# HGRN layer: one tile of i's projection moved into each of the first seven state tiles

## What is computed

```
def hgrn2_mixer(h, w_in, lb, onorm_g, w_out):       # H = 8 heads of 128, chunks C = 64
    q, fl, i, g = split(h @ w_in, 4)
    q = silu(q); f = lb + (1 - lb) * sigmoid(fl); k = 1 - f; logf = log(f)
    b = cumsum(logf, within a chunk)
    q_dec, k_inv, k_state = q * exp(b), k * exp(-b), k * exp(b_last - b)
    A = causal(q_dec @ k_inv.T)                      # scores, 64 x 64 in a chunk
    o_intra = A @ i                                  # products from the scores
    U = k_state.T @ i                                # state products
    S_next = exp(b_last) * S + U                     # state updates, chunk after chunk
    o = o_intra + q_dec @ S                          # products with the states
    o = o * rsqrt(mean(o * o) + eps) * onorm_g       # over the 128 values of a head
    return (o * silu(g)) @ w_out
```

## Time and profile before

| | us |
|---|---|
| median of three runs | 3572.93 (3567.02 to 3577.70) |
| the profiled execution | 3579.63 |
| its span, first to last instruction | 3577.8 |
| PE busy | 3427.7 (96%) |
| DVE busy | 1945.3 (54%) |
| ACT busy | 1275.9 (36%) |

### The profile page before, as it was taken

How to read it: one execution, slowest core, us unless ns; L and a number is a source line. 1 busy time by engine, 2 the same in 40 slices (tenths; PEclk the granted TensorE clock), 3 DMA queues, 4 the chain that set the end, 5 groups by cost and what they waited for, 6 DMA issues and landing times.

```text
span 3577.8 us, 54525 instructions
## 1 busy us (share of the span) xinstructions
PE 3427.7 (96%) x22697; PEld 2834.6 (79%) x22697; DVE 1945.3 (54%) x2638; ACT 1275.9 (36%) x1638; POOL 13.9 (0%) x20
## 2 busy tenths in 40 slices
PE   9999999999999999899999999999899887999998
PEld 7778888887788878677887788887887885888887
DVE  4566636436574654575344665344676666755434
ACT  3474424334443332353222443223532113633223
POOL 0000000000000000000000000000000000000000
PEclk9999999999899999999999999999999999999999
DMA  4102222221122222112222222222234001123222
GB/s 158 59 1 94 96 101 96 94 94 48 55 99 94 94 94 97 59 59 94 95 94 94 94 71 94 94 96 92 94 106 142 16 5 45 54 83 104 96 94 71
DMA packets 50429, 297.06 MB, mean 83 GB/s; under 512 B 6847, under 2 KB 7871, under 8 KB 17348
## 3 DMA queue, kind: packets, MB, share of 16 engines
q1 hardware_dynamic: 39376, 269.92, 22.1%
q10 hardware_dynamic: 10868, 24.41, 1.9%
HBM read 283.99 MB, written 10.33 MB: 82 GB/s over the span
## 4 chain that ended last, share of the span: by engine, by line
PE 85%; DVE 9%; ACT 4%; issue 2%; ACTq 0%; DMA 0%; DVEq 0%
PE PS L353 13%; PE PS L355 13%; PE PS L354 13%; PE PS L478 7%; PE PS L480 7%; PE PS L479 7%; PE PS L2153 2%; PE PS L2154 2%; PE PS L2155 2%; PE PS L2678 1%; PE PS L2681 1%; PE PS L2671 1%; PE PS L3170 1%; PE PS L3171 1%; PE PS L3172 1%
## 5 line engine op out<-in xcount | busy, mean ns | idle before, releaser
L172 DVE TENSOR_TENSOR WL<-W,WH 128x2048 fp32r<-128x2048 f32 x249 | 570.6, 2292 | 681.2 <-ACT WH L162 675.6
L162 ACT ACTIVATE WH<-W 128x2048 fp32r<-128x2048 f32 x249 | 476.3, 1913 | 1058.5 <-PE PS L480 553.8
L353 PE MATMUL PS<-XH,WH 128*128 128x512 f32 x2080 | 812.8, 391 | 4.2 <-issue 4.2
L355 PE MATMUL PS<-XH,WL 128*128 128x512 f32 x2080 | 810.2, 389 | 0.0
L354 PE MATMUL PS<-XL,WH 128*128 128x512 f32 x2080 | 810.1, 389 | 0.0
L353 PEld LDWEIGHTS PS<-XH,WH 128*128 128x128 f32 x2080 | 390.9, 188 | 91.1 <-issue 10.6
L354 PEld LDWEIGHTS PS<-XL,WH 128*128 128x128 f32 x2080 | 390.9, 188 | 81.8 <-issue 1.0
L355 PEld LDWEIGHTS PS<-XH,WL 128*128 128x128 f32 x2080 | 390.8, 188 | 81.2
L752 DVE TENSOR_TENSOR PS<-PS,R 128x512 f32<-128x512 f32 x248 | 171.0, 696 | 432.4 <-PE PS L355 422.7
L478 PE MATMUL PS<-HH,WH 128*128 128x512 f32 (+1 forms) x960 | 374.8, 390 | 1.2
L480 PE MATMUL PS<-HH,WL 128*128 128x512 f32 (+1 forms) x960 | 373.8, 389 | 0.0
(11 more groups left out here) (509 smaller groups left out, 4761.7 us busy)
## 6 DMA issues: line engine op xcount, KB each, us to landing
W<-in_weights SPq DMA_DIRECT2D x254, 1024.0 KB, 4.9
gate_spill<-slots ACTq DMA_DIRECT2D x16, 256.0 KB, 2.0
gates<-gate_spill ACTq DMA_DIRECT2D x2, 2048.0 KB
x_spill<-X ACTq DMA_DIRECT2D x1, 2048.0 KB, 7.8
X<-x_spill ACTq DMA_DIRECT2D x1, 2048.0 KB
out<-X ACTq DMA_DIRECT2D x8, 256.0 KB, 2.1
W<-in_weights SPq DMA_DIRECT2D x2, 512.0 KB, 5.3
X<-in_x ACTq DMA_DIRECT2D x4, 256.0 KB, 7.7
```

What stands on the lines that cost most here:

```text
L162: P.e.activation(K.WH[:, s, :], K.W[:, s, :], ACT.Copy).then_inc(P.sem("hi_ready"), P.adds("hi_ready"))
L172: P.e.tensor_tensor(K.WL[:, s, :], K.W[:, s, :], K.WH[:, s, :].bitcast(F32), ALU.subtract).then_inc(P.sem("weights_split"), P.adds("weight ...
L353: P.e.matmul(out, wh[:, k, c], xh[:, k, r], start=(k == 0), stop=False)
L355: last = P.e.matmul(out, wl[:, k, c], xh[:, k, r], start=False, stop=(k == KT - 1))
```

## The change

The stages `Store` for i and `Hgrn` become one stage, `HgrnHalf`. Its PE program begins with one tile of i's projection (`AHEAD = 8` steps of three matmuls). Then come the eight state tiles. The table `FILL` says for each state tile how many steps stand at five places in it; for the first seven tiles it is eight steps at the third place, between the state products and the products from the scores. For this the rest is put in another order:

- i's projection has two banks of its own (1 and 4), each used again for every second tile; `scaled` on DVE takes the finished tile and only then makes the next tile's keys.
- PE turns over the keys first, then multiplies the scores, then takes the mean, and only then turns over i, in the bank in which the scores stood, so behind their mask. The keys and the mean share bank 2.
- ACT takes the output of a tile at the start of the next one, squares first, then copies; it copies the keys before i.
- Norm, high and low part of the output come one tile behind instead of two.
- The weight panels are split at the end of every second state tile (`panel_end`). The first tile's scan, exponentials and keys are no longer made ahead of the stage.
- The logs have one row instead of eight, and the output's high and low part lie in other memory (`o_hi`, `o_lo`), since XH and XL are still read.

The core of the diff:

```
-class Hgrn(Stage):
-    tiles_given = 8
+class HgrnHalf(Wide):
+    between_panels = True
+    tiles_given = 8
+    DENSE, MEANS = (1, 4), 2
+    FILL = ((0, 0, 8, 0, 0),) * 7 + ((0, 0, 0, 0, 0),)
+    AHEAD = 8
...
     def dve(self, K, P):
+        def scaled(j):
+            P.e.wait_ge(P.sem("tile_done"), P.due("tile_done"))
+            P.e.tensor_tensor(K.i1[:, j, :], K.PS[:, self.DENSE[j % 2], 0:S], K.RB[:, :], ALU.mult).then_inc(P.sem(f"tile_evacuated{j % 2}"), 1)
...
+        decays(0)
+        keys(0)
+        scaled(0)
         for t in range(8):
-            if t >= 2:
-                normed(t - 2)
+            masked(t)
             if t < 7:
                 decays(t + 1)
-            masked(t)
-            if t >= 2:
-                low_part(t - 2)
+            if t:
+                normed(t - 1)
             states(t)
             if t < 7:
+                scaled(t + 1)
                 keys(t + 1)
+            if t:
+                low_part(t - 1)
+            if t % 2 == 0:
+                panel_end()
...
     def act(self, K, P):
+        logs(0)
+        exps(0)
         logs(1)
         for t in range(8):
+            if t:
+                taken(t - 1)
             turned(t)
-            if t >= 2:
-                high_part(t - 2)
-            if t >= 1:
+            if t:
                 root(t - 1)
             if t < 7:
                 exps(t + 1)
             if t < 6:
                 logs(t + 2)
-            taken(t)
+            if t:
+                high_part(t - 1)
+            if t % 2 == 0:
+                panel_end()
...
     def pe(self, K, P):
+        def fill(steps):
+            for _ in range(steps):
...
+                if k == 0:
+                    if t == 0:
+                        P.e.wait_ge(P.sem("weights_split"), P.due("weights_split"))
+                    P.e.wait_ge(P.sem(f"tile_evacuated{t}"), P.due(f"tile_evacuated{t}", less=-1 if p else 0))
...
+                P.e.matmul(out, wh[:, k, c], K.XH[:, k, 0:S], start=(k == 0), stop=False)
+                P.e.matmul(out, wh[:, k, c], K.XL[:, k, 0:S], start=False, stop=False)
+                last = P.e.matmul(out, wl[:, k, c], K.XH[:, k, 0:S], start=False, stop=(k == KT - 1))
...
+        fill(self.AHEAD)
         for t in range(8):
...
-            for c in tiles:
-                last = P.e.transpose(K.PS[:, 0, c], K.i1[:, t, c], K.ident[:, :])
-            last.then_inc(P.sem("iT_done"), P.adds("iT_done"))
             P.e.wait_ge(P.sem("keys_ready"), P.due("keys_ready"))
+            if t >= 2:
+                P.e.wait_ge(P.sem("o_root"), P.due("o_root"))
...
             last.then_inc(P.sem("A_done"), P.adds("A_done"))
-            P.e.wait_ge(P.sem("iT_ready"), P.due("iT_ready"))
+            fill(fills[0])
             P.e.wait_ge(P.sem("ksT_ready"), P.due("ksT_ready"))
+            if t:
+                means(t - 1)
+            P.e.wait_ge(P.sem("A_ready"), P.due("A_ready"))
+            input_there(t)
+            for c in tiles:
+                last = P.e.transpose(K.PS[:, 0, c], K.i1[:, t, c], K.ident[:, :])
+            last.then_inc(P.sem("iT_done"), P.adds("iT_done"))
+            fill(fills[1])
+            P.e.wait_ge(P.sem("iT_ready"), P.due("iT_ready"))
...
             last.then_inc(P.sem("U_done"), P.adds("U_done"))
+            fill(fills[2])
             if t:
-                means(t - 1)
-            P.e.wait_ge(P.sem("A_ready"), P.due("A_ready"))
+                P.e.wait_ge(P.sem("o_taken"), P.due("o_taken"))
...
+            fill(fills[3])
             P.e.wait_ge(P.sem("states_ready"), P.due("states_ready"))
...
             last.then_inc(P.sem("o_done"), P.adds("o_done"))
+            fill(fills[4])
```

More of the change, by code:

```diff
@@ L1348, in decays @@
         P.e.wait_ge(P.sem("logf_ready"), P.due("logf_ready"))
-        P.e.tensor_tensor_scan(K.h_b[:, :], K.reset64[:, :], self.log_row(K, t), 0.0, ALU.mult, ALU.add).then_inc(P.sem("b_ready"), P.adds("b_ready"))
+        P.e.tensor_tensor_scan(K.h_b[:, :], K.reset64[:, :], K.lf[:, :], 0.0, ALU.mult, ALU.add).then_inc(P.sem("b_ready"), P.adds("b_ready"))
     def keys(self, K, P, t):
@@ L1360, in keys, with panel_end @@
         P.e.tensor_tensor(ks, ki, ends, ALU.mult).then_inc(P.sem("keys_ready"), P.adds("keys_ready"))
[L1362 to L1384, removed]
     def dve(self, K, P):
         decays, keys = lambda t: self.decays(K, P, t), lambda t: self.keys(K, P, t)
+        def scaled(j):
+            P.e.wait_ge(P.sem("tile_done"), P.due("tile_done"))
+            P.e.tensor_tensor(K.i1[:, j, :], K.PS[:, self.DENSE[j % 2], 0:S], K.RB[:, :], ALU.mult).then_inc(P.sem(f"tile_evacuated{j % 2}"), 1)
+        def panel_end():
+            split_dve(K, P)
+            P.split_left -= 1
+            P.count("tile_evacuated0", 1)
+            P.count("tile_evacuated1", 1)
+            P.parity ^= 1
         def masked(t):
             P.e.wait_ge(P.sem("A_done"), P.due("A_done"))
-            P.e.tensor_tensor(K.aT[:, :], K.PS[:, 4, 0:256], K.causal64[:, 0:256], ALU.mult).then_inc(P.sem("A_ready"), P.adds("A_ready"))
+            P.e.tensor_tensor(K.aT[:, :], K.PS[:, 0, 0:256], K.causal64[:, 0:256], ALU.mult).then_inc(P.sem("A_ready"), P.adds("A_ready"))
         def states(t):
@@ L1445, in root @@
             P.e.wait_ge(P.sem("o_mean"), P.due("o_mean"))
-            P.e.activation(r, K.PS[:, 1, :], ACT.Ln, bias=K.eps_col[:, 0:1]).then_inc(P.sem("act_order"), P.adds("act_order"))
+            P.e.activation(r, K.PS[:, self.MEANS, :], ACT.Ln, bias=K.eps_col[:, 0:1]).then_inc(P.sem("act_order"), P.adds("act_order"))
             P.e.wait_ge(P.sem("act_order"), P.due("act_order", 0))
@@ L1452, in taken, with panel_end @@
             for u in range(2):
-                P.e.activation(K.halves(K.o_sq[:, t % 2, :], u), K.halves_ps(u), ACT.Square)
+                last = P.e.activation(K.halves(K.o_sq[:, t % 2, :], u), K.halves_ps(u), ACT.Square)
+            last.then_inc(P.sem("squares_ready"), P.adds("squares_ready"))
+            for u in range(2):
                 last = P.e.activation(K.halves(K.f1[:, t, :], u), K.halves_ps(u), ACT.Copy)
-            last.then_inc(P.sem("squares_ready"), P.adds("squares_ready"))
+            last.then_inc(P.sem("o_taken"), P.adds("o_taken"))
         def high_part(t):
             P.e.wait_ge(P.sem("o_gated"), P.due("o_gated"))
-            P.e.activation(K.XH[:, t, 0:S], K.f1[:, t, :], ACT.Copy).then_inc(P.sem("o_hi"), P.adds("o_hi"))
+            P.e.activation(K.o_hi[:, t, :], K.f1[:, t, :], ACT.Copy).then_inc(P.sem("o_hi"), P.adds("o_hi"))
+        def panel_end():
+            P.e.wait_ge(P.sem("tile_done"), P.due("tile_done", 2))
+            split_act(K, P)
+            P.split_left -= 1
+            P.count("tile_evacuated0", 1)
+            P.count("tile_evacuated1", 1)
+            P.parity ^= 1
+        P.e.preload_act_table_set("natural_log_exp_and_others")
+        for t in range(2):
+            P.e.wait_ge(P.sem(f"tile_evacuated{t}"), P.due(f"tile_evacuated{t}", 0, less=-2))
+        logs(0)
+        exps(0)
         logs(1)
         for t in range(8):
+            if t:
+                taken(t - 1)
             turned(t)
-            if t >= 2:
-                high_part(t - 2)
-            if t >= 1:
+            if t:
                 root(t - 1)
@@ L1496, in pe @@
             for n, half, j, c in chunks:
-                last = P.e.matmul(K.PS[half, 4, 64 * j:64 * j + 64], K.h_ki[:, b, c], K.h_qd[:, b, c], start=True, stop=True)
+                last = P.e.matmul(K.PS[half, 0, 64 * j:64 * j + 64], K.h_ki[:, b, c], K.h_qd[:, b, c], start=True, stop=True)
             last.then_inc(P.sem("A_done"), P.adds("A_done"))
+            fill(fills[0])
+            P.e.wait_ge(P.sem("ksT_ready"), P.due("ksT_ready"))
+            if t:
[6 more added lines that the diff above has]
+            fill(fills[1])
             P.e.wait_ge(P.sem("iT_ready"), P.due("iT_ready"))
-            P.e.wait_ge(P.sem("ksT_ready"), P.due("ksT_ready"))
             for n, half, j, c in chunks[:7]:
@@ L3623, in program @@
         for st, after in pairs:
-            if isinstance(st, Store) and isinstance(after, (ForgettingAttention, Hgrn, DiffAttention)):
+            if isinstance(st, Store) and isinstance(after, (ForgettingAttention, DiffAttention)):
                 st.owe, st.next_act, st.next_dve = True, after.ahead_act, after.ahead_dve
```

60 lines of the change are left out of this document (45 added, 15 removed).

## The result

| | before | changed |
|---|---|---|
| median of 12 runs each | 3573.39 (3567.02 to 3577.70) | 3580.91 (3578.85 to 3582.32) |
| the profiled execution | 3579.63 | 3578.85 |
| its span | 3577.8 | 3577.1 |

The ratio is 1.0022, with a 95% interval from 1.0014 to 1.0029: the changed kernel is slower by 5 to 10 us. That is real, and inside the 0.3% that was called no change. The forecast of 3573 was 8 us too low. The two profiled executions, however, differ by 0.8 us the other way, near the -0.4 of the prediction's sum.

A forecast was written before the change was run, and what follows sets the result against it. PE, busy nearly throughout, was taken as the bound, with gains only from its waits or low clock. Tiles -5.3, entry +5.0 and exit -0.1 gave -0.4, so the median 3572.9 became 3572.5, said as 3573; range 3564 less 2 to 3588.

The forecast's parts named there:

- no change: Whole kernel: a difference within 0.3%, 10.7 us, can't be told; chance 0.70, against 0.20 slower and 0.10 faster.
- the prediction's sum: Whole stage: -5.3 for the tiles, +5.0 for the entry, -0.1 for the exit, together -0.4 us.
- Entry: Stage start to first tile's output: PE waits 4.7 for first keys, then low clock; 26.6 against 21.6, a 5.0 loss.
- bound of 824.2: Stage start: when the first tile's products are out if the clock stays full throughout, instead of 828.4.
- Filled tile: State tiles holding a tile of i: 13.75 each, 1.5 of it waiting, states hidden by 2.2.
- Last tile and exit: Last state tile without i: 13.4, norm and states exposed, low clock; then 3.5 to the output projection at 927.8.
- A: Slower: two waits ahead of the state products drop the clock in every filled tile, 2.5 each, 15: 3588; chance 0.18.
- B: Faster: PE never leaves the full clock, at entry, last tile and exit; -9, 3564; chance 0.12.
- C: Filled tiles: DVE makes keys 0.5 late in each, +3.5: 3576; chance 0.62 together with the main forecast.
- D: Filled tiles: states not hidden because DVE reaches them too late, up to 1.5 more each, 3583; chance 0.08.
- the old order's own luck with the clock: State tiles before the change: clock luck worth 4 us, counted within the 0.20 chance for slower.

The follow-up runs named there:

- e6_entry: Changed kernel plus four unread products between the first tile of i and the wait for the first keys: 3577.20, ratio 1.0021.
- e3_both: Changed kernel with 16 steps of i ahead and the rest as one step at each short wait, five (once four) behind the state products: 3562.34, ratio 0.9977.
- e5_early: Changed kernel with the tile of i behind the scores instead of behind the state products: 3617.12 (two runs), ratio 1.0134.
- e7_best: e3_both with, in the last state tile, states updated before the older output's norm and one unread product ahead of the states' wait: 3559.09, ratio 0.9969.
- e4_busy: Kernel before, with one unread 128x512 product in each state tile ahead of the wait for the states: 3562.81, ratio 0.9976.

## Why the prediction was right, and where it was not

**Entry.** Predicted: a wait of 4.7, the first tile at half clock, first output at 828.4. Measured: 4.85, clock 0.50 from 810.42 to 820.66, output taken at 828.22, in an execution in which the stage began 0.5 us earlier than before (801.36 instead of 801.83), so 26.9 after its start instead of 26.6. `e6_entry` confirms the low clock's share, 3.5 us against the 4.2 between the prediction's 828.4 and its bound of 824.2.

**Filled tile.** Predicted 13.75 with waits of 0.7 and 0.75, states hidden by 2.2 us, a tie at the keys. Measured 13.87, 0.73 and 0.69, 2.6, and keys 0.3 us ahead of PE. `e3_both` shows that filling the waits gives 1.0 to 1.4 of the 1.42 that they last, and `e5_early` that the place hides the states.

**Last tile and exit.** Predicted 13.4 and 3.5, with the output projection at 927.8. Measured 13.09 and 3.1, at 927.70, 0.4 later than forecast if counted from the stage's start.

**The rivals.** A did not happen: 99 us at 1.00 over six filled tiles with two short waits in each. The rule of the Trainium skill cited for it ("TensorE: Matmul & The Clock Gate", "A second HAM failure mode: psum-queue depth-cycling"), that short idles between groups of matmuls make the clock swing, is thus not borne out by the changed kernel's waits of 0.7, and is by the old order's waits of up to 1.9 us; the page gives no length for such an idle, so `e5_early` with its 3.3 us doesn't test it. B's condition, no low clock anywhere, did not come about by itself; `e7_best` had to make it, covering the waits as well. C's tie held. D did not occur.

**The failed step** is the one from the sum to the time: "The profiled execution took 3579.6 ..., above all three timed runs; by the change alone it would be 3579.2, and the median 3572.9 becomes 3572.5." It carried the 6.7 us by which the profiled execution stood above the median over to the changed kernel. Part of that 6.7 was the very stretch that the change rewrites: this execution's layer of 126.7 was the longest of five, 2.5 above their mean of 124.2. The new order has its low clock at two fixed places, so its layer is 126.5 to 126.8 in all three profiled executions, and there was no such luck to carry over: its own profiled execution is 2.1 *below* its median. That the two layers of the first pair agree within 0.2 us, as the sum had it, is in this sense luck. The prediction put "the old order's own luck with the clock, which is worth 4 us" into the chances for slower, where it belonged in the sum: a layer of the mean length would have given a loss of 2.4 and a forecast of about 3575, one of 120 to 123 a loss of 4 to 6 and a forecast of 3577 to 3579.

That is 2 to 6 of the 8 us. About 3 more are seen in the scan, a stretch that the prediction took as unchanged without naming it; they go with the idle time of PE there, whose cause stays open. That the timed medians (5 to 10 us by the interval) lie further apart than the 4.2 between the means of the profiled executions fits the clocks of the timed runs, and is argued from them, not tested. The forecast of no change that can be told was right, because the change exchanges the old order's waits and low clock for short waits, an entry and a last tile that cost about as much, by these estimates a few us more.

## What to carry to other kernels

Where one profiled execution stands well above the median and the stretch that is changed contains low clock, take that stretch's typical length as the base before an edit is worth a few us: profile several executions of the kernel before, and compare their mean granted clock with that of the timed runs. Work moved into waits gains what it covers, but check what it had covered at the place that it leaves; here the first keys cost 5 us, and only two tiles ahead, a step at each short wait and another order and one unread product in the last tile turned 0.2% slower into 0.3% faster. And where PE waits for a microsecond or two in each round of a loop, a product that nobody reads may be worth more than a better order: try it first.

## What was not expected of the hardware

- One unread 128x512 product in fp32, 1.06 us long, in each state tile of some 9 us kept the clock at 1.00 throughout the layer and gained 7.6 us (`e4_busy`).
- Two waits of 0.73 and 0.69, with 1.6 us of work between them, left the clock at 1.00 in the changed kernel; one of 1.52 in a tile without projection matmuls was followed by 0.50. One of 1.44 at the entry of `e6_entry`, behind projection matmuls and four unread products, left it at 1.00.
- The same instructions in the same order take 120.3 to 126.7 us in five executions of the old order, with low stretches that come at other places and with other lengths; the layers of the new order agree within 0.3 us.
- The scan takes 360.6 to 368.6 us over fourteen executions. The time at the low clock (20.6 to 24.8 us) does not go with it; idle time of PE without a releaser in the profile (1.8 to 9.9 us) does, and in the changed kernel it stands twice in each of seven rounds.
